# Tile 0's products of the spatially gated layer transposed by VectorE in 32 by 32 squares

## The reference, cut to what matters

```python
def _gmlp_mixer(x, g_norm, w_in, g_sgu, w_s, b_s, w_out):
    h = _rms_norm(x, g_norm)
    z = jax.nn.gelu(h @ w_in, approximate=False)
    u, v = jnp.split(z, 2, axis=-1)               # 256 x 2048 each
    v = _rms_norm(v, g_sgu)
    v = v.reshape(b, s // A_CHUNK, A_CHUNK, A_GROUPS, A_GROUP_DIM)
    ...
    v = jnp.einsum('gij,bnjgc->bnigc', w, v) + b_s.T[None, None, :, :, None]
    v = v.reshape(b, s, A_DFF)
    return (u * v) @ w_out
```

## Time and profile before

| | us |
|---|---|
| median of 3 runs | 1172.41 |
| lowest and highest run | 1171.55, 1172.63 |
| the profiled execution's own time | 1172.13 |
| its span in the profile | 1170.3 |
| PE busy | 1160.1 (99%) |
| DVE busy | 842.7 (72%) |
| ACT busy | 598.8 (51%) |

### The profile page before, as it was taken

How to read it: one execution, slowest core, us unless ns; L and a number is a source line. 1 busy time by engine, 2 the same in 40 slices (tenths; PEclk the granted TensorE clock), 3 DMA queues, 4 the chain that set the end, 5 groups by cost and what they waited for, 6 DMA issues and landing times.

```text
span 1170.3 us, 15455 instructions
## 1 busy us (share of the span) xinstructions
PE 1160.1 (99%) x6009; PEld 968.7 (83%) x6009; DVE 842.7 (72%) x1438; ACT 598.8 (51%) x797; POOL 59.8 (5%) x109
## 2 busy tenths in 40 slices
PE   8999999999999999999999999999999999999998
PEld 7888888888889988888888888888898787888887
DVE  6666577988857768798886665545568877979874
ACT  7744454544355555454445454434567867545441
POOL 1100010000000000000002400000110001000000
PEclk9999999999999999999999999999999999999999
DMA  7744536555445433655443665455355141565540
GB/s 289 288 155 156 210 113 246 216 216 201 173 167 180 149 140 144 243 224 216 186 176 144 239 230 199 177 199 199 122 204 199 38 144 73 196 236 216 216 144 37
DMA packets 34691, 213.58 MB, mean 182 GB/s; under 512 B 4666, under 2 KB 6842, under 8 KB 10042
## 3 DMA queue, kind: packets, MB, share of 16 engines
q1 hardware_dynamic: 34617, 212.59, 49.0%
HBM read 211.53 MB, written 1.05 MB: 182 GB/s over the span
## 4 chain that ended last, share of the span: by engine, by line
PE 96%; DVE 2%; ACT 1%; DMA 0%; POOL 0%; issue 0%; SPq 0%; DVEq 0%; POOLq 0%
PE ps L325 30%; PE ps L327 29%; PE ps L326 29%; PE ps L331 3%; DVE wlo L1559 1%; PE ps L797 1%; PE ps L848 1%; PE ps L669 1%; PE ps L825 0%; DMA raw<-in_w_v 0%; PE ps L649 0%; DVE tmp L1578 0%; ACT whi L1086 0%; PE ps L772 0%; PE ps L858 0%; DVE a_s L1770 0%
## 5 line engine op out<-in xcount | busy, mean ns | idle before, releaser
L1559 DVE TENSOR_TENSOR wlo<-raw,whi 128x2048 fp32r<-128x2048 f32 (+2 forms) x196 | 432.9, 2233 | 62.6 <-ACT whi L1086 62.5
L1086 ACT ACTIVATE whi<-raw 128x2048 fp32r<-128x2048 f32 (+2 forms) x196 | 363.4, 1869 | 124.6 <-DMA raw<-in_w_gu 69.6
L325 PE MATMUL ps<-whi,xThi 128*128 128x512 f32 (+2 forms) x960 | 373.0, 389 | 1.7 <-DVE wlo L1559 0.9
L327 PE MATMUL ps<-whi,xTlo 128*128 128x512 f32 (+2 forms) x960 | 370.7, 386 | 0.0
L326 PE MATMUL ps<-wlo,xThi 128*128 128x512 f32 (+2 forms) x960 | 370.4, 386 | 0.0
L325 PEld LDWEIGHTS ps<-whi,xThi 128*128 128x128 f32 x960 | 180.3, 188 | 39.8 <-DVE wlo L1559 2.2
L327 PEld LDWEIGHTS ps<-whi,xTlo 128*128 128x128 f32 x960 | 180.3, 188 | 36.6
L326 PEld LDWEIGHTS ps<-wlo,xThi 128*128 128x128 f32 x960 | 180.4, 188 | 35.4
L1691 DVE STREAM_TRANSPOSE f_sil<-f_hid 32x128 f32<-32x128 f32 x480 | 145.3, 303 | 10.0 <-DVE f_hid L1683 0.9
L1201 ACT ACTIVATE f_sil<-ps,stats 128x256 f32<-128x256 f32 x88 | 40.7, 470 | 213.6 <-PE ps L327 212.8
L325 PE MATMUL ps<-whi,f_hThi 128*128 128x512 f32 x352 | 139.9, 397 | 0.0
(11 more groups left out here) (289 smaller groups left out, 1180.8 us busy)
## 6 DMA issues: line engine op xcount, KB each, us to landing
raw<-in_w_gu SPq DMA_DIRECT2D x88, 1024.0 KB, 4.9
raw<-in_w_dn SPq DMA_DIRECT2D x44, 1024.0 KB, 5.4
raw<-in_w_u SPq DMA_DIRECT2D x8, 1024.0 KB, 5.8
raw<-in_w_ao SPq DMA_DIRECT2D x8, 1024.0 KB, 5.1
raw<-in_w_v SPq DMA_DIRECT2D x6, 1024.0 KB, 5.0
raw<-in_w_bv SPq DMA_DIRECT2D x4, 1024.0 KB, 5.1
raw<-in_w_bk SPq DMA_DIRECT2D x4, 1024.0 KB, 4.8
raw<-in_w_bq SPq DMA_DIRECT2D x4, 1024.0 KB, 4.8
```

The costliest lines, as they stand in the source:

```text
L325: e.matmul(ps, a[0], b[0], start=start, stop=False)
L327: return e.matmul(ps, a[1], b[0], start=False, stop=stop)
L1086: e.activation(dst[:, cs], raw_cols(i, cs), ACT.Copy).then_inc(*inc("whi", i, p))
L1559: e.tensor_tensor(lo[:, cs], raw_cols(i, cs), hi[:, cs].bitcast(F32), ALU.subtract).then_inc(*inc("wlo", i, p))
```

## The change

Tile 0's four transposing steps move from PE to DVE. DVE writes them, square by square, into the first 512 columns of the scratch buffer `junk`, with 16 instructions of 32 partitions x 128 numbers, and from there ACT and DVE make the `hi` and `lo` parts. Tile 1's stay with PE and `PS[3]`.

```diff
-            def u_turn(c, t):
-                e.wait_ge(*at("uv", c, t))
-                if c or t:
-                    e.wait_ge(*at("uvlo", *((c, 0) if t else (c - 1, 1))))
-                turn(XB[1], [ub[t][:, 128 * i:128 * i + 128] for i in range(4)], "uv", c, t)
+            def u_turn(c):
+
+                e.wait_ge(*at("uv", c, 1))
+                if c:
+                    e.wait_ge(*at("uvlo", c - 1, 1))
+                turn(XB[1], [ub[1][:, 128 * i:128 * i + 128] for i in range(4)], "uv", c, 1)
...
                 u_project(c, 1, pair)
-                u_turn(c, 0)
...
-                e.wait_ge(*(at("turned", "uv", c - 1, t) if c else at("vlo", 3, t)))
+                e.wait_ge(*(at("turned" if t else "uvturn", "uv", c - 1, t) if c else at("vlo", 3, t)))
...
-                e.wait_ge(*at("turned", "uv", c, t))
+                e.wait_ge(*at("turned" if t else "uvturn", "uv", c, t))
...
-                copy(flat(uvT[t][0]), PS[XB[1]][:, :], "uvhi", c, t)
+                copy(flat(uvT[t][0]), PS[XB[1]][:, :] if t else junk[:, 0:512], "uvhi", c, t)
...
+            def u_turn(c):
+
+                a, b = (v.rearrange("p (k n) -> p k n", k=4) for v in (ub[0][:, :], junk[:, 0:512]))
+                e.wait_ge(*at("uv", c, 0))
+                for i in range(4):
+                    for j in range(4):
+                        m = e.transpose(b[32 * j:32 * j + 32, :, 32 * i:32 * i + 32], a[32 * i:32 * i + 32, :, 32 * j:32 * j + 32])
+                m.then_inc(*inc("uvturn", "uv", c, 0))
...
-                evac_lo([flat(a) for a in uvT[t]], PS[XB[1]][:, :], "uvhi", "uvlo", c, t)
+                evac_lo([flat(a) for a in uvT[t]], PS[XB[1]][:, :] if t else junk[:, 0:512], "uvhi", "uvlo", c, t)
...
                     lo(c - 1, 1)
+                u_turn(c)
                 gate(c, 1)
```

More of the change, by code:

```diff
@@ L486, in gmlp @@
                 if c > 0:
-                    u_turn(c - 1, 1)
+                    u_turn(c - 1)
                     dn = [take(), take()]
@@ L490, in gmlp @@
                 u_project(c, 1, pair)
-                u_turn(c, 0)
                 if c > 0:
                     downs(c - 1, 1, dn, c == 1)
-            u_turn(3, 1)
+            u_turn(3)
             dn = [take(), take()]
```

## The result

The changed kernel takes 1173.89 us (median of 20 runs), the kernel before 1172.3 (median of 20 runs taken beside it): a ratio of 1.0016, with a 95% interval of 1.001 to 1.0022. So it is slower by about 1.6 us. The interval leaves out no change; a loss of 0.2% still lies within it. The forecast was 1173.9, in a range of 1171.9 to 1175.6. The profiled execution took 1173.91, its span is 1171.9 against 1170.3.

What follows compares the result with a forecast made beforehand. PE was taken to bound the kernel, busy for 99% of the span. A delay of 2.84 us in chunk 0 less 1.32 saved in chunks 1 to 3 gave + 1.5 us on 1172.41, so 1173.9 us, range 1171.9 to 1175.6.

Steps and rivals of the forecast that it cites:

- PE's saving, 0.44 a turn: On PE's list: each turn of four transposes removed spares 0.44 us, 1.76 for four if PE finds no new wait.
- The block: On DVE: 16 transposes of 32 partitions by 128 float32 numbers take 5.05 us in each of four chunks.
- The estimate from the Trainium skill: DVE transposes: 311 ns read as a whole square's price gives 1.24 us a step; the prediction used the trace's 5.05 instead.
- Chunk 0's delay: Chunk 0: the block holds up tile 1's gate and unit 15, so PE falls 2.84 us behind; ends 1.7 and 3.3.
- Chunks 1 to 3: DVE's block is covered by its wait for PE's next mix, so each chunk saves PE 0.44 us, 1.32 together.
- The queues: SP's loads of units 18 and 19 move from 72.61 to 78.0 and 80.2 us, with their landing hidden.
- The clock: Rival, chunk 0's sparse stretch: TensorE's clock falls to 1.2 GHz, costing 2.9 us over 5.7 us, for 1176.8; chance 0.08.
- The words on ACT's queue: Chunk 0: called "the queueing that matters", ACT doing nothing between 67 and 73 us though unit 15 is in its buffer.
- The length up to which PE keeps the whole saving: Rival that the block is cheap or hidden, 1170.7 us: needs a block of at most 2.3 us; chance 0.06.
- PE's waits: Chunk 0, between 72 and 78 us: PE's waits for DVE (`spm`, `uv`, `uvlo`, `wlo`) sum to about 3.2 us.
- The chance of 0.75: Whole kernel: probability that the measured time is the same within about 0.2%, 2.3 us; faster 0.03, slower 0.22.

Runs made afterwards that it cites:

- none: Against the kernel before: tile 0's transposes left out on both engines, its products used untransposed, so the output differs; 1170.33 us, ratio 0.9985.
- keep0: Against the changed kernel: tile 0's turn moves to DVE in chunks 1 to 3 only and stays on PE in chunk 0; 1170.72 us.
- only0: Against the changed kernel: tile 0's turn moves to DVE in chunk 0 only, chunks 1 to 3 stay as before the change; 1175.1 us.
- act_first: Against the changed kernel: in chunk 0 ACT rounds units 15 and 16 ahead of `hi` (0,0) instead of behind it; 1173.54 us.
- half: Against the changed kernel: each DVE block is 8 transposes instead of 16, the other squares left out, so the output differs; 1171.23 us.

## Why the prediction was right

**PE's saving, 0.44 a turn.** Right: 1.76 for four (`none`), 1.33 for three (keep0, forecast 1.32).

**The block.** Forecast as 5.05 us by the feed-forward layers' block, measured 5.04. The estimate from the Trainium skill (VectorE: DVE Perf Modes, The three transpose paths), 1.24 us for a step, is far off for float32 in pieces of 32 partitions: the 64 pieces took 303 ns each, near the 311 that the Trainium skill gives for 128 x 128 in bf16, and four of them make one square. No run here transposes bf16.

**Chunk 0's delay.** Forecast 2.84, measured 2.93 (only0). In this trace the mix (0,0) starts 0.13 us later than in that of the kernel before (60.06 against 59.93). With that, the forecast instants were 73.36, 73.89 and 78.14 for the block's end, unit 15's rounding and PE's seventh matmul, and the rows have 73.35, 73.92 and 78.20. Of the 0.06 at the end, 0.03 are ACT's `hi` from `junk`: 0.53 from its start to the next one's, where that from the bank had 0.50.

**Chunks 1 to 3.** DVE was forecast to have 1.3 and 2.7 us to spare behind the block; the rows show 1.33 and 2.83. PE has no wait there.

**The queues.** SP's loads of units 18 and 19 were forecast to move from 72.61 to 78.0; they went out at 78.17, and nothing waited for them.

**The clock.** It stayed at 1.00 though PE was busy for only 5.57 of 8.00 us, with waits of up to 1.54 us, so that rival did not come about. The advice that the prediction takes for it from the Trainium skill (TensorE: Matmul & The Clock Gate) stands there in the section Why this matters for your kernels, not in the one that the prediction names.

**What was not right.** Some things, none of which moved the sum. The words on ACT's queue gave it a weight that it does not have: 0.33 of 2.9 us (act_first); DVE's own list would have held unit 15 nearly as long. The length up to which PE keeps the whole saving is about 1.8 us and not 2.3 (an estimate from `half`). PE's waits were to sum to about 3.2 us; its list has 1.5 and 0.9, because it counts from the end of the matmul before, and two of the four waits do not show in it at all. By the starts they come to about 3.1: 1.70 for `spm`, 0.11 for `uv`, 0.24 for `uvlo` and 1.06 for unit 15. The chance of 0.75 for "within 0.2%" was borne out, but narrowly: + 0.16% lies near its edge. And the prediction took 0.2% for the least that can be told from no change; with 20 runs on either side, 0.16% could be told from it.

**Luck.** That 1173.89 meets the forecast of 1173.9 to the last digit is closer than the working can promise. The rise was forecast as 1.52 and is 1.58 by the stage and 1.59 by the medians, and the three runs that it was added to had a median 0.11 above that of the 20 beside the change.

## What to carry to other kernels

Before moving work from the bound engine to one that is idle for over a quarter of the time, lay the new instructions into that engine's list at their place and follow what stands behind them: three blocks in front of a wait were free here, and one block in front of work that the bound engine wanted 7 us later cost its full length less what was to spare. Where such a step repeats, price each repetition apart; leaving out the one that does not fit turned + 1.6 us into - 1.4. And a small loss or gain, of a microsecond in a thousand, is better read as the distance between two of the bound engine's own instructions than from the whole time.

## What the runs showed of the hardware

Nothing that was not expected. Of use for others: DVE's transpose of 32 partitions by 128 float32 numbers takes 303 ns at the median in the feed-forward layers (298 to 311) and here (289 to 308), where in chunks 1 to 3 PE multiplies beside it without a break; and PE's granted clock stayed at 1.00 through a stretch of 8 us in which PE was busy for 5.57.
